# TensorE sums the first norm's squares, two end-gate outputs move into the first projection, and a modulation slab, the taps and two slab splits change places

## The chip, the cores and the metric

The kernel runs on one core of one Trainium2 chip. The metric is device time in microseconds (us), the median of several executions. Before the change it is 727.38 us, the median of three (727.26 to 727.83). The engines named below are TensorE (PE; PEld is its weight load), VectorE (DVE), ScalarE (ACT), GpSimd (POOL), and SyncE (SP), whose queue issues nearly all transfers.

## The reference, cut to what matters

Two stacks of two layers each run one after the other on x of 256 rows by 1024 columns, all in float32. The parts that the change touches are the first layer, the modulation vectors of the layers behind it, and the convolution with its layer norm in the second stack:

```python
shift, scale, gate = jnp.split(cs @ mod_w[layer] + mod_b[layer], 3, axis=-1)   # cs = silu(c)
h = _modulate(_rmsnorm(x, norm_g[layer]), shift, scale)        # the first norm: squares of x summed by row
u, g = jnp.split(h @ w_in, 2, axis=-1)                         # first projection u, end gates g
u = lax.conv_general_dilated(u, conv_w[:, None, :], ...) + conv_b          # 4 taps
r  = sigmoid(_block_diag(u, w_a) + b_a)                        # head gates
gi = sigmoid(_block_diag(u, w_x) + b_x)
log_a = -8 * r * softplus(-lam); a = exp(log_a)
b_in = sqrt(-expm1(2 * log_a)) * (gi * u)
_, hs = associative_scan(_lin_combine, (a, b_in), axis=1)
x = x + gate * ((hs * silu(g)) @ w_out)
# then: keys and values from x, queries and attention gates from x (second modulation), attention, output
# second stack, first layer (a Fourier mixer beside a gated convolution):
u = v * jax.nn.sigmoid(gate)
u = lax.conv_general_dilated(u, conv_w[:, None, :], ...) + conv_b          # 31 taps, 512 channels
u = silu(layernorm(u.reshape(b, s, 4, 128), ...))              # four channel tiles of 128
y = jnp.concatenate([ya, yb], axis=-1) @ w_out_ab
# then two gated feed-forward blocks (2816 wide) with a pooling mixer between them, and a last norm
```

## The kernel before, in words

A tile is 128 channels by 256 positions; x is eight of them (`X`). The program is written by hand, one instruction stream for each engine, with semaphores between them, and each stream runs in the order in which it is written. Nothing is scheduled by a tool.

**Weights.** They come as slabs of 1 MB or less (128 partitions by up to 2048 numbers) in the order of `PLAN`, which `slab_plan` (L19) writes. SP issues them in that order on one queue (L591 to L617). Slabs named in `OWN` (u, g, the two head matrices, y: the whole first layer) have places of their own. All others go through a ring of five buffers `raw`: a slab is issued only when the slab five places before it in the ring has been used up. While SP waits for that, all slabs behind it wait too. There are three kinds of ring slabs:
- "first": the two modulation vectors of the first layer. DVE multiplies the two halves of a slab with silu(c) and sums them (`first_sums`, L1071, two instructions over 1024 numbers each).
- "mod" (`MODS`): a piece of another modulation vector, read in the same way by `mod_sum` and `stream`. Numbers 0 to 3 are the first layer's output gate, 4 to 11 the keys' and values' modulation, 12 to 19 the query side's (alternately the factor and the shift), 20 to 23 the second layer's gate.
- matrices (`MATS`): each is split in a high and a low part. ACT copies it to the high part (L665), then DVE subtracts to get the low part (L1068, over 2048 numbers), and TensorE uses both in three products (L1638 to L1640). `stream(upto)` on ACT and on DVE works off the plan up to a slab at that place in the engine's own order; DVE does the mod slabs on its way, too.

**The first norm and the first projection.** ACT squares X into `F1` (L717 for four tiles, L720 for two and two). DVE adds the eight tiles to one (semaphore `s_n0`), TensorE sums that over its channels with two matmuls of one column (L1731), ACT takes the root, DVE the inverse (`c0`, L1197), TensorE spreads it over a tile (L1706), ACT copies it to `RS` (L665). Then, for each of the eight tiles kt, DVE multiplies X (`first_tile`), sums the "first" slab (`first_sums`) and closes it (`first_close`); ACT makes H(kt) (L728); TensorE uses H(kt) for all eight outputs u at once, with one slab for each kt (L1710). Matmuls on `ones`, whose results nobody reads, stand in the waits ahead (`idle_products`, L1715).
The end gates g 0 and 1 follow in banks of their own (`end_gates(0)`), then the head gates (16 outputs), the end gates 2 to 7, and the output projection y. Banks are given out in `outputs`. On DVE the softplus of lambda (`s_sp`), the 4-tap convolution (24 instructions, semaphore `s_conv`), the mod slabs 0 to 7, the recurrence, the mod slabs 8 to 11 and the first two matrix splits follow in that order. A head gate needs the convolution of its two tiles of u.

**Keys, values and queries.** DVE adds y to X tile by tile (L1071, `x<-pb,mv,x`) and gathers the squares for the second norm. TensorE starts the keys before that norm is known, and sums the norm's squares after the fourth kt of them (L1815), its inverse is spread after the sixth. Then come key inputs, value inputs and query inputs on ACT and DVE, between matrix splits and mod slabs.

**The convolution with 31 taps.** Three of its four channel tiles are made on DVE, 30 instructions each (`pump`, list `taps`; each reads and writes the same tile), the fourth on TensorE with diagonal matrices. Layer norm of the four tiles is done in steps between TensorE (`ln_mean`, `ln_var`, `ln_row`), ACT (`ln_square`, `ln_root`, `ln_high`) and DVE (`ln_centre`, `ln_inverse`, `ln_scale`, `ln_low`), tile 3 first. TensorE's product with `w_out_ab` (`mixed`, `both`) goes on between these steps as far as its inputs are there.

## Time and profile before

| | us |
|---|---|
| median of three runs | 727.38 |
| the profiled execution, own time | 727.91 |
| its span, first to last instruction | 726.1 |
| PE busy | 710.1 |
| PEld busy | 617.9 |
| DVE busy | 498.4 |
| ACT busy | 396.8 |
| POOL busy | 12.2 |
| longest chain, share that runs over PE / DVE | 81% / 14% |

The profiled execution took 1.8 us more than its span, for what lies around the program. The kernel moves 158.4 MB. A fp32 matmul is recorded as two instructions on PE, so a matmul of 256 columns has two records. The mean length of a matmul record says little, since matmuls overlap; the distance between starts is what counts.

### The profile page before, as it was taken

To read this page: it belongs to the slowest core of one execution; us is meant where nothing else is said; L and a number is where in the kernel's file an instruction comes from. 1 tells how busy PE (TensorE), PEld (TensorE's weight loads), DVE (VectorE), ACT (ScalarE), POOL (GpSimd) and SP (SyncE) were. 2 spreads that over 40 slices of the span, in tenths; PEclk is the share of its full clock that TensorE was granted. 3 is DMA by queue.
4 is the path that set the end of the run, shared out by engine and by line. 5 is a ranking of instruction groups with operands and counts; after the bars stand their busy time and mean duration, and the time that the engine had idled before them with its cause. 6 is when DMAs were issued, how large, how long until landed. Compare 5 with 4: busy or idle time off the path is not lost.

```text
span 726.1 us, 9536 instructions
## 1 busy us (share of the span) xinstructions
PE 710.1 (98%) x3812; PEld 617.9 (85%) x3812; DVE 498.4 (69%) x799; ACT 396.8 (55%) x616; POOL 12.2 (2%) x18
## 2 busy tenths in 40 slices
PE   6999999999999999989999999999999999999996
PEld 5888889979899999878888888888888888888885
DVE  5889996998877889966755454554776455454544
ACT  3156545964885778768643444334755443444423
POOL 0000000000310000000000000000000000000000
PEclk8999999999999999999999999999999999999999
DMA  8999994799836349433755455445236554455101
GB/s 334 416 421 422 420 400 164 250 388 341 352 117 232 118 174 265 142 116 135 287 211 178 175 196 205 178 174 181 109 116 231 196 203 181 176 190 207 67 1 58
DMA packets 23468, 158.40 MB, mean 218 GB/s; under 512 B 2624, under 2 KB 2880, under 8 KB 5248
## 3 DMA queue, kind: packets, MB, share of 16 engines
q1 hardware_dynamic: 22464, 152.82, 55.8%
q0 software_dynamic: 960, 4.98, 2.5%
q8 instruction: 30, 0.49, 0.3%
q14 instruction: 14, 0.11, 0.0%
HBM read 156.74 MB, written 1.05 MB: 217 GB/s over the span
## 4 chain that ended last, share of the span: by engine, by line
PE 81%; DVE 14%; ACT 2%; DMA 2%; issue 1%; SPq 0%; DVEq 0%
PE pb L1638 20%; PE pb L1640 20%; PE pb L1639 20%; PE pb L1710 13%; DVE f L1071 5%; DVE w L1068 3%; DVE raw L1071 3%; PE pb L2063 1%; DVE f L1068 1%; DMA raw<-w_dram 1%; PE pb L2131 1%; DVE r L1068 1%; PE pb L1985 1%; DMA x<-x_dram 1%; PE pb L1715 0%
## 5 line engine op out<-in xcount | busy, mean ns | idle before, releaser
L1068 DVE TENSOR_TENSOR w<-raw,w 128x2048 fp32r<-128x2048 f32 x95 | 216.9, 2290 | 141.4 <-ACT w L665 141.4
L665 ACT ACTIVATE w<-raw 128x2048 fp32r<-128x2048 f32 x99 | 188.5, 1914 | 144.9 <-PE pb L1640 114.7
L1638 PE MATMUL pb<-w,r 128*128 128x512 f32 (+1 forms) x608 | 238.9, 393 | 0.2 <-DVE r L1068 0.2
L1640 PE MATMUL pb<-w,r 128*128 128x512 f32 (+1 forms) x608 | 235.4, 387 | 0.0
L1639 PE MATMUL pb<-w,r 128*128 128x512 f32 (+1 forms) x608 | 235.0, 387 | 0.0
L1640 PEld LDWEIGHTS pb<-w,r 128*128 128x128 f32 x608 | 114.1, 188 | 23.7
L1638 PEld LDWEIGHTS pb<-w,r 128*128 128x128 f32 x608 | 114.2, 188 | 23.0 <-DVE r L1068 0.6
L1639 PEld LDWEIGHTS pb<-w,r 128*128 128x128 f32 x608 | 114.4, 188 | 22.2
L1638 PE MATMUL pb<-r,w 128*128 128x256 f32 x288 | 82.4, 286 | 1.5 <-DVE r L1068 1.0
L1640 PE MATMUL pb<-r,w 128*128 128x256 f32 x288 | 81.5, 283 | 0.0
L1639 PE MATMUL pb<-r,w 128*128 128x256 f32 x288 | 81.5, 283 | 0.0
L1071 DVE SCALAR_TENSOR_TENSOR raw<-raw,acc 128x1024 f32<-128x1024 f32 x64 | 75.1, 1219 | 4.0 <-DMA raw<-w_dram 4.0
L1638 PEld LDWEIGHTS pb<-r,w 128*128 128x128 f32 x288 | 55.2, 192 | 2.3 <-DVE w L1068 2.3
L1710 PE MATMUL pb<-h,ow 128*128 128x256 f32 x256 | 56.4, 383 | 0.0
L1710 PEld LDWEIGHTS pb<-h,ow 128*128 128x128 f32 x256 | 49.4, 193 | 7.0
L1639 PEld LDWEIGHTS pb<-r,w 128*128 128x128 f32 x288 | 55.2, 192 | 0.0
L1640 PEld LDWEIGHTS pb<-r,w 128*128 128x128 f32 x288 | 55.2, 192 | 0.0
L1002 ACT ACTIVATE t<-pb,rn 128x256 f32<-128x256 f32 x44 | 20.7, 476 | 59.7 <-PE pb L1640 59.6
L1071 DVE SCALAR_TENSOR_TENSOR f<-f,vec 128x256 f32<-128x256 f32 x114 | 46.4, 476 | 0.3
L1071 DVE SCALAR_TENSOR_TENSOR t<-pb,rn,t 128x256 f32<-128x256 f32 x44 | 21.1, 483 | 22.8 <-ACT t L1002 22.8
L1710 PE MATMUL pb<-t,ow 128*128 128x256 f32 x128 | 27.8, 379 | 0.0
L1710 PEld LDWEIGHTS pb<-t,ow 128*128 128x128 f32 x128 | 24.3, 190 | 3.3
(215 smaller groups left out, 667.4 us busy)
## 6 DMA issues: line engine op xcount, KB each, us to landing
raw<-w_dram SPq DMA_DIRECT2D x129, 1024.0 KB, 5.0
ow<-w_dram SPq DMA_DIRECT2D x8, 1024.0 KB, 14.8
ow<-w_dram SPq DMA_DIRECT2D x8, 512.0 KB, 16.5
oh<-w_dram SPq DMA_DIRECT2D x2, 1024.0 KB, 22.4
w<-w_dram POOLq DMA_DIRECT2D x2, 1024.0 KB, 14.5
x<-x_dram SPq DMA_DIRECT2D x2, 512.0 KB, 5.5
f<-rc_dram POOLq DMA_DIRECT2D x1, 1024.0 KB, 5.1
acc<-row_dram POOLq DMA_DIRECT2D x2, 512.0 KB, 4.8
```

Of the source, the lines that this page charges most:

```text
L665: return e.activation(out, in_, ACT.Copy, **kw)
L1002: e.activation(tt[(at_ - 1) % 4][:, :], bank_of("gu", layer, i, a)[:, 0:T], ACT.Silu, scale=rn[:, 2 * layer, a:a + 1]).then_inc(s_sgt, 1)
L1068: return e.tensor_tensor(out, a, b, op)
L1071: return e.scalar_tensor_tensor(out, a, s, b, op0, op1, **kw)
L1638: e.matmul(out, a_hi, b_hi, start=start, stop=False)
L1639: e.matmul(out, a_hi, b_lo, start=False, stop=False)
L1640: return e.matmul(out, a_lo, b_hi, start=False, stop=stop)
L1710: return e.matmul(out, slab[:, o:o + P], rhs, start=start, stop=stop)
L1985: done = e.transpose(bank_of("tx", n, a, m)[:, j * P:j * P + P], Xt[:, a, o:o + P], ident)
L2063: done = e.transpose(out[:, j * T + a * P:j * T + a * P + P], tt[4 + (at_ - 1) % 4][:, j * P:j * P + P], ident)
L2131: done = e.matmul(bank_of("p", a, c)[:, g % 2 * 256:g % 2 * 256 + 256], rc[:, b, g, a * P:a * P + P], Q[:, b, g, :], start=b == 0, stop=b ...
```

## The change

Five edits, all in the order of work; the arithmetic done on each weight stays the same.

1. The first norm: DVE's four additions of squares are gone (with `s_n0`). TensorE sums all eight squared tiles itself, with 16 matmuls of one column instead of 2; two of the idle matmuls ahead of it go. DVE takes the inverse before it sums the first "first" slab, not between that slab's halves, and the second half is summed behind `first_tile(0)`.
2. The slab of g 0 and 1 is cut in two parts. The part for kt 0 to 2 comes behind the third pair of slabs, and TensorE does these six matmuls behind kt 2 of the first projection; the part for kt 3 to 7 comes behind the last u slab, and its ten matmuls stand within kt 7, between the outputs u 5 and u 6. The outputs g 0 and g 1 lie in the free halves of the banks of u 6 and u 7. The head gates follow on u 7 at once.
3. The slab of mod 0 comes ahead of the two head matrices in the plan, and DVE sums it ahead of the 4-tap convolution.
4. The slabs of mod 12 and mod 13 come ahead of matrix slabs 2 and 3. DVE sums mod 12 ahead of the addition of y 7 and mod 13 ahead of matrix split 2; matrix split 3 is done before the wait for the second norm instead of behind the eight multiplications with it.
5. The 31 taps: the third tile's taps join the round of three from its third place on, so that at the end two taps on one tile stand in a row. `ln_inverse(3)` stands behind the eighth of the 15 taps that are left after `ln_centre(3)`, not behind all of them; `ln_scale(3)` and matrix split 28 come ahead of `ln_centre` of tiles 0 to 2. On TensorE the sums `ln_mean` of tiles 0 to 2 all stand behind `both(2)`.

```diff
@@ slab_plan
     for kt in range(KT):
         plan.extend([("first", "mod_w", 0, kt), ("u", "rg_w_in", 0, kt)])
-    plan.extend([("g", "rg_w_in", 0, 0), ("heads", "rg_w_a", 0), ("heads", "rg_w_x", 0)])
+        if kt == EARLY - 1:
+            plan.append(("part", "rg_w_in", 0, 0))
+    plan.append(("part", "rg_w_in", 0, EARLY))
+    at = len(plan)
     mod("mod_w", 0, 2)
+    plan[at + 1:at + 1] = [("heads", "rg_w_a", 0), ("heads", "rg_w_x", 0)]
...
-    weave(kv(512, D) + values + cols("att_w_in", 0, 512), [("mod", "mod_w", 1, unit, j) for j in range(4) for unit in (1, 0)],
-          [0, 2, 3, 3, 4, 5, 7, 7])
+    late = [("mod", "mod_w", 1, unit, j) for j in range(4) for unit in (1, 0)]
+    plan.extend(late[0:2])
+    weave(kv(512, D) + values + cols("att_w_in", 0, 512), late[2:], [3, 3, 4, 5, 7, 7])
@@ outputs
-    o.out(*run("u", *range(8)))
-    o.place(1, ("g", 0))
-    o.place(2, ("g", 1))
-    o.finish(("g", 0), ("g", 1))
-    rest = [3, 4, 5, 6, 7, 0]
+    o.hold(*run("u", *range(8)))
+    for b in range(2):
+        o.place(o.bank["u", 6 + b], ("g", b))
+    o.finish(*run("u", *range(6)))
+    o.finish(("g", 0), ("g", 1), ("u", 6), ("u", 7))
+    rest = [1, 2, 3, 4, 5, 6]
@@ taps
-        taps = [(d, j) for j in range(8) for d in (0, 1)]
-        taps += [x for j in range(8, 31) for x in ((0, j), (1, j), (2, j - 8))] + [(2, j) for j in range(23, 31)]
+        taps = [(d, j) for j in range(2) for d in (0, 1)]
+        taps += [x for j in range(2, 31) for x in ((0, j), (1, j), (2, j - 2))] + [(2, 29), (2, 30)]
@@ vector
-            two = F1[:, 0:2, :]
-            p.wait_ge(s_sq0, 1)
-            tt_(two, two, F1[:, 2:4, :], ADD).then_inc(s_n0, 1)
             for c in range(2):
                 p.wait_ge(*ended("sc", c))
                 e.tensor_copy(silu_c[:, c * 512:c * 512 + 512], bank_of("sc", c)[:, :]).then_inc(s_silu, 1)
-            for n in range(1, 3):
-                p.wait_ge(s_sq0, n + 1)
-                p.wait_ge(s_n0, n)
-                tt_(two, two, F1[:, 2 * n + 2:2 * n + 4, :], ADD).then_inc(s_n0, 1)
-            p.wait_ge(s_n0, 3)
-            tt_(F1[:, 0, :], F1[:, 0, :], F1[:, 1, :], ADD).then_inc(s_n0, 1)
+            p.wait_ge(s_rt, 1)
+            e.reciprocal(c0[:, :], c0[:, :]).then_inc(s_rc0, 1)
             p.wait_ge(s_xb, 16)
             first_sums(0, [0])
-            p.wait_ge(s_rt, 1)
-            e.reciprocal(c0[:, :], c0[:, :]).then_inc(s_rc0, 1)
-            first_sums(0, [1])
             p.wait_ge(s_rs, 1)
             first_tile(0)
+            first_sums(0, [1])
             first_close(0)
...
+            stream(MODS[0])
             p.wait_ge(s_pad, 1)
             for c in range(4):
...
-            stream(MODS[0])
+            stream(MODS[1])
             for d in range(8):
                 if d in (2, 4, 6):
-                    stream(MODS[d // 2])
+                    stream(MODS[1 + d // 2])
...
             for d in range(8):
+                if d == 7:
+                    stream(MODS[12])
                 p.wait_ge(*ended("y", d))
...
             add(7)
+            stream(MODS[13])
             stream(MATS[2])
             p.wait_ge(s_rt, 2)
             e.reciprocal(c1[:, :], c1[:, :]).then_inc(s_rc1, 1)
-            stream(MODS[12])
+            stream(MATS[3])
...
-            stream(MATS[3])
             key(0, 1, 2, 3)
...
-            stream(MODS[13])
             key(4, 5)
...
             pump(78 - tap_n["n"])
             ln_centre(3)
+            pump(8)
+            ln_inverse(3)
             pump(len(taps) - tap_n["n"])
-            ln_inverse(3)
+            ln_scale(3)
+            stream(MATS[28])
             ln_centre(0)
             ln_centre(1)
-            ln_scale(3)
-            stream(MATS[28])
+            ln_centre(2)
             ln_low(3)
-            ln_centre(2)
             stream(MATS[29])
@@ tensor
-            idle_products(4)
+            idle_products(2)
             bank_free("n", 0)
-            p.wait_ge(s_n0, 4)
-            for a in range(2):
-                done = e.matmul(bank_of("n", 0)[:, a:a + 1], F1[:, 0, a * P:a * P + P], ones_sb[:, 0:1], start=True,
-                                stop=True)
+            for kt in range(KT):
+                p.wait_ge(s_sq0, max(1, kt // 2))
+                for a in range(2):
+                    done = e.matmul(bank_of("n", 0)[:, a:a + 1], F1[:, kt, a * P:a * P + P], ones_sb[:, 0:1],
+                                    start=kt == a == 0, stop=kt == KT - 1 and a == 1)
...
+            def early_gates(part, kts):
+
+                slab, there = own("part", part)
+                p.wait_ge(*there)
+                for b in range(2):
+                    for kt in kts:
+                        done = plain(out_of("g", b), slab, (kt - part) * 256 + b * P, H(kt), False, False)
+                    if kts[-1] == KT - 1:
+                        done.then_inc(s_ps, 1)
...
                 for d in range(8):
+                    if kt == KT - 1 and d == 6:
+                        early_gates(EARLY, range(EARLY, KT))
...
+                if kt == EARLY - 1:
+                    early_gates(0, range(EARLY))
...
-            end_gates(0)
...
             both(1)
             ln_row(3)
-            ln_mean(0, (s_tap, tap_at[0, 30]))
-            ln_mean(1, (s_tap, tap_at[1, 30]))
             both(2)
+            for d in range(3):
+                ln_mean(d, (s_tap, tap_at[d, 30]))
             mixed(3, 0, 0, 1)
-            ln_mean(2, (s_tap, tap_at[2, 30]))
             mixed(3, 1, 0, 1)
```

What moves is seen in the order of DVE's instructions at three places. In these rows `raw,mv<-raw,acc ... x2` is the sum of one mod slab, `w<-raw,w` the low part of one matrix slab. First, around the 4-tap convolution (`f<-f,vec ... x24`), before and then now:

```order
51 L1227 TENSOR_SCALAR sm<-sm 128x8
52 L1228 TENSOR_SCALAR sm<-sm 128x8
53 L1071 SCALAR_TENSOR_TENSOR f<-f,vec 128x256 x24
54 L1071 SCALAR_TENSOR_TENSOR raw,mv<-raw,acc 128x1024 x2
55 L1068 TENSOR_TENSOR f<-f,t 128x256 x2
```

```order
48 L1230 TENSOR_SCALAR sm<-sm 128x8
49 L1231 TENSOR_SCALAR sm<-sm 128x8
50 L1083 SCALAR_TENSOR_TENSOR raw,mv<-raw,acc 128x1024 x2
51 L1083 SCALAR_TENSOR_TENSOR f<-f,vec 128x256 x24
52 L1083 SCALAR_TENSOR_TENSOR raw,mv<-raw,acc 128x1024 x2
53 L1080 TENSOR_TENSOR f<-f,t 128x256 x2
```

One mod slab is now summed ahead of the convolution. Second, from the end of the addition of y to the first multiplications with the second norm (`f<-x,rs`), before and then now:

```order
96 L1071 SCALAR_TENSOR_TENSOR r<-x,mv,kr 128x256
97 L1068 TENSOR_TENSOR na<-na,sq 128x256
98 L1071 SCALAR_TENSOR_TENSOR r<-x,mv,kr 128x256
99 L1068 TENSOR_TENSOR na<-na,sq 128x256
100 L1068 TENSOR_TENSOR w<-raw,w 128x2048
101 L1315 RECIPROCAL c<-c 128x2
102 L1071 SCALAR_TENSOR_TENSOR raw,mv<-raw,acc 128x1024 x2
103 L1068 TENSOR_TENSOR mv<-mv,vec 128x2
104 L1071 SCALAR_TENSOR_TENSOR mv<-mv,vec 128x2
105 L1068 TENSOR_TENSOR f<-x,rs 128x256 x8
106 L1068 TENSOR_TENSOR w<-raw,w 128x2048
```

```order
95 L1083 SCALAR_TENSOR_TENSOR mv<-mv,vec 128x2
96 L1083 SCALAR_TENSOR_TENSOR x<-pb,mv,x 128x256
97 L1083 SCALAR_TENSOR_TENSOR r<-x,mv,kr 128x256
98 L1080 TENSOR_TENSOR na<-na,sq 128x256
99 L1083 SCALAR_TENSOR_TENSOR r<-x,mv,kr 128x256
100 L1080 TENSOR_TENSOR na<-na,sq 128x256
101 L1083 SCALAR_TENSOR_TENSOR raw,mv<-raw,acc 128x1024 x2
102 L1080 TENSOR_TENSOR mv<-mv,vec 128x2
103 L1080 TENSOR_TENSOR w<-raw,w 128x2048
104 L1322 RECIPROCAL c<-c 128x2
105 L1080 TENSOR_TENSOR w<-raw,w 128x2048
106 L1080 TENSOR_TENSOR f<-x,rs 128x256 x8
```

Mod 12 (its last instruction is row 95) is ahead of the last addition, mod 13 ahead of the inverse, and a second split has come ahead of the eight multiplications. Third, the end of the taps and tile 3's layer norm (`lnr` is its inverse, `f<-pb,f` is `ln_centre`), before and then now:

```order
262 L1071 SCALAR_TENSOR_TENSOR f<-pb,f 128x256
263 L1071 SCALAR_TENSOR_TENSOR f<-f,vec 128x256 x15
264 L1488 RECIPROCAL lnr<-lnr 128x2
265 L1071 SCALAR_TENSOR_TENSOR f<-pb,f 128x256 x2
266 L1071 SCALAR_TENSOR_TENSOR f<-f,vec,pb 128x256
267 L1068 TENSOR_TENSOR w<-raw,w 128x2048
```

```order
260 L1083 SCALAR_TENSOR_TENSOR f<-pb,f 128x256
261 L1083 SCALAR_TENSOR_TENSOR f<-f,vec 128x256 x8
262 L1493 RECIPROCAL lnr<-lnr 128x2
263 L1083 SCALAR_TENSOR_TENSOR f<-f,vec 128x256 x7
264 L1083 SCALAR_TENSOR_TENSOR f<-f,vec,pb 128x256
265 L1080 TENSOR_TENSOR w<-raw,w 128x2048
266 L1083 SCALAR_TENSOR_TENSOR f<-pb,f 128x256 x3
```

The inverse has moved seven taps up.

## Rows read from the trace of the kernel before

**Rows 1.** The page, part 1: busy us, share of the span, instructions.
```profile
PE 710.1 (98%) x3812; PEld 617.9 (85%) x3812; DVE 498.4 (69%) x799; ACT 396.8 (55%) x616; POOL 12.2 (2%) x18
```

**Rows 2.** By stretch: length; PE, PEld, DVE, ACT, POOL busy; clock, DMA share, GB/s.
```profile
0.00:20.00 20.00, 14.12 (x49) 11.49 (x50) 12.13 (x30) 7.03 (x11) 0.19 (x4) 0.83 0.89 343
20.00:40.00 20.00, 20.00 (x95) 17.60 (x94) 15.82 (x38) 3.00 (x5) 0.00 (x0) 1.00 1.02 418
140.00:200.00 60.00, 58.02 (x392) 53.07 (x391) 56.01 (x100) 39.57 (x69) 5.89 (x6) 1.00 0.92 356
300.00:340.00 40.00, 38.01 (x196) 31.42 (x195) 30.50 (x65) 26.47 (x52) 0.53 (x1) 1.00 0.36 127
340.00:726.00 386.00, 379.94 (x1757) 315.60 (x1755) 209.80 (x203) 179.59 (x202) 0.00 (x0) 1.00 0.46 166
```

**Rows 3.** Timeline, 6 to 16 us: start, length, engine, line, operation [idle before].
```profile
6.73 1.06 ACT L717 ACTIVATE f<-x 128x1024 f32<-128x1024 f32 x1 [2.01 <-DMA x<-x_dram]
...
11.62 1.01 PE L1731 MATMUL pb<-ones_sb,f 128*128 128x1 f32 x4 [4.56 <-DVE f L1068]
...
12.67 0.26 ACT L722 ACTIVATE c<-pb,vec 128x2 f32<-128x2 f32 x1 [3.51 <-PE pb L1731]
...
15.29 0.60 ACT L728 ACTIVATE h<-f,mv 128x256 f32<-128x256 f32 x1 [0.76 <-DVE mv L1071]
```

**Rows 4.** Timeline of PEld, the same stretch.
```profile
11.62 0.93 PEld L1731 LDWEIGHTS pb<-ones_sb,f 128*128 128x128 f32 x4 [4.96 <-DVE f L1068]
...
16.05 1.19 PEld L1710 LDWEIGHTS pb<-h,ow 128*128 128x128 f32 x3
```

**Rows 5.** Busy time by 1 us, columns as in rows 2.
```profile
11.00:12.00 1.00, 0.38 (x2) 0.38 (x3) 0.97 (x3) 0.00 (x0) 0.00 (x0) 0.69 0.98 410
...
18.00:19.00 1.00, 1.00 (x5) 0.83 (x5) 1.00 (x4) 0.60 (x1) 0.00 (x0) 0.90 1.11 463
```

**Rows 6.** Timeline of PE at 318 us: matmuls of one column.
```profile
318.30 1.39 PE L1968 MATMUL pb<-ones_sb,t 128*128 128x1 f32 x12
```

**Rows 7.** Timeline of DVE, 37 to 56 us.
```profile
37.55 1.22 DVE L1071 SCALAR_TENSOR_TENSOR raw<-raw,acc 128x1024 f32<-128x1024 f32 x1 [0.74 <-DMA raw<-w_dram]
...
45.69 9.58 DVE L1071 SCALAR_TENSOR_TENSOR f<-f,vec 128x256 f32<-128x256 f32 x24
...
55.19 1.22 DVE L1071 SCALAR_TENSOR_TENSOR raw<-raw,acc 128x1024 f32<-128x1024 f32 x1
```

**Rows 8.** Timeline of PE at 51 us: the first head gates.
```profile
51.87 5.34 PE L1710 MATMUL pb<-f,oh 128*128 128x256 f32 x24
```

**Rows 9.** Timeline of DVE, 114 to 139 us.
```profile
114.23 0.48 DVE L1071 SCALAR_TENSOR_TENSOR x<-pb,mv,x 128x256 f32<-128x256 f32 x1 [2.24 <-PE pb L1710]
...
120.86 1.21 DVE L1071 SCALAR_TENSOR_TENSOR raw<-raw,acc 128x1024 f32<-128x1024 f32 x1
...
123.92 2.77 DVE L1068 TENSOR_TENSOR f<-x,rs 128x256 f32<-128x256 f32 x8 [0.31 <-ACT rs L665]
...
135.02 1.21 DVE L1071 SCALAR_TENSOR_TENSOR raw<-raw,acc 128x1024 f32<-128x1024 f32 x1
...
138.17 2.28 DVE L1068 TENSOR_TENSOR w<-raw,w 128x2048 fp32r<-128x2048 f32 x1
```

**Rows 10.** Timeline of ACT at 135 us: the high part of matrix slab 5.
```profile
135.47 1.90 ACT L665 ACTIVATE w<-raw 128x2048 fp32r<-128x2048 f32 x1
```

**Rows 11.** Timeline of PEld at 160 us: the first query weights.
```profile
160.69 0.19 PEld L1638 LDWEIGHTS pb<-r,w 128*128 128x128 f32 x1 [1.41 <-DVE w L1068]
```

**Rows 12.** Timeline of DVE, 272 to 312 us: taps, and tile 3's centre.
```profile
272.73 17.10 DVE L1071 SCALAR_TENSOR_TENSOR f<-f,vec 128x256 f32<-128x256 f32 x43
...
304.08 7.02 DVE L1071 SCALAR_TENSOR_TENSOR f<-f,vec 128x256 f32<-128x256 f32 x15
```

**Rows 13.** Timeline of ACT at 306 us: the root for tile 3.
```profile
306.60 0.26 ACT L945 ACTIVATE lnr<-pb,vec 128x2 f32<-128x2 f32 x1 [0.68 <-PE pb L1968]
```

**Rows 14.** Timeline of PE at 311 us: tile 3's row.
```profile
311.23 0.43 PE L1706 MATMUL pb<-cst,lnr 128*128 128x128 f32 x2 [1.80 <-DVE lnr L1488]
```

More of the change, by code:

```diff
@@ L15 @@
 RT = 8
+EARLY = 3
 def slab_plan():
@@ L97 @@
 PLAN = slab_plan()
-OWN = [i for i, p in enumerate(PLAN) if p[0] in ("u", "g", "y") or p[0] == "heads" and p[1] != "pool_map_2"]
+OWN = [i for i, p in enumerate(PLAN) if p[0] in ("u", "part", "g", "y") or p[0] == "heads" and p[1] != "pool_map_2"]
 RING = [i for i in range(len(PLAN)) if i not in OWN]
@@ L113, in width @@
 def width(i):
+    if PLAN[i][0] == "part":
+        return (KT - EARLY if PLAN[i][3] else EARLY) * 256
     return PLAN[i][4] * 256 if PLAN[i][0] == "mat" else D if PLAN[i][0] == "u" else 2048
@@ L403, in two_block_program @@
             sem(f"s_{n}") for n in ("ones", "pad", "gg", "cs", "silu", "lam", "sp", "one", "gain", "mv"))
-        s_sq0, s_n0, s_rc0 = sem("s_sq0"), sem("s_n0"), sem("s_rc0")
+        s_sq0, s_rc0 = sem("s_sq0"), sem("s_rc0")
         s_sq, s_na, s_rt, s_rs, s_rtc, s_rcl, s_rsb, s_xn = (
@@ L463, in two_block_program @@
             own_at["u", kt] = OW[:, kt // 4, kt % 4 // 2, o_:o_ + D]
+        own_at["part", 0] = OW[:, 2, 0, 0:EARLY * 256]
+        own_at["part", EARLY] = OW[:, 2, 0, EARLY * 256:2048]
         for c in range(4):
-            own_at["g", c] = OW[:, 2 + c // 2, c % 2, :]
+            if c:
+                own_at["g", c] = OW[:, 2 + c // 2, c % 2, :]
             own_at["y", c] = OW[:, c // 2, c % 2, :]
@@ L481, in out_of @@
         def out_of(*name):
+            if name in (("g", 0), ("g", 1)):
+                return PB[OUT.bank[name]][:, T:2 * T]
             return PB[OUT.bank[name]][:, 0:T]
@@ L2172 @@
     for i, p in enumerate(plan):
+        if p[0] == "part":
+            k0, k1 = (EARLY, KT) if p[3] else (0, EARLY)
+            m = a[p[1]][p[2]][k0 * P:k1 * P, D:D + 256]
+            w[i, :, 0:(k1 - k0) * 256] = m.reshape(k1 - k0, P, 256).transpose(1, 0, 2).reshape(P, -1)
+            continue
         if p[0] in ("first", "u", "g", "y"):
```

## The prediction

> **What bounds the kernel now.** I read the page first: TensorE is busy for 710.1 of 726.1 us [rows 1]. So an edit pays only if it shortens TensorE's work, which none of these does, or one of its 16 us of idle time. The busy time by stretch shows where they lie: 5.9 us in the first 20, 2.0 between 140 and 200, 2.0 between 300 and 340, 6.1 behind 340 [rows 2]. The last are the output's tail behind the last matmul and the change does not touch them. The timelines of the other three stretches tell what ends each idle time, and every edit lands in one of them.
> At the start TensorE waits 4.56 us for DVE's additions of squares, and its granted clock falls to half (mean 0.69 in 11 to 12 us, 0.90 in 18 to 19, so half from about 11.4 to 18.2 us) [rows 3, 5]. At 160 us it waits 1.41 us for a matrix split of DVE, which in 140 to 200 us is busy 56 of 60 us [rows 2, 11]. At 311 us it waits 1.80 us for the inverse that DVE makes behind 15 taps [rows 12, 14]. Between these places TensorE is never idle, so what is won at one is carried to the next.
>
> **Edit 1, the first norm.** The squares of the first four tiles are done at 7.79 us [rows 3]. DVE's additions go. TensorE has 16 matmuls of one column, 32 instructions. At full clock twelve such take 318.30 to about 319.56, 0.105 us each [rows 6], so 32 take 3.4 us; at half clock four loads take 0.8 us (0.93 with the last one's tail), 0.20 each, so 6.4 us [rows 4]. Those are the two ends. I take full clock, since the idle time ahead of them shrinks: TensorE was idle from 7.06 us; with two idle matmuls fewer (four instructions of about 0.22 us [rows 8]) it is idle from 6.2 to 7.8, that is 1.6 us in place of 4.56 [rows 3].
> The sum then ends at 11.4 instead of 12.63 us, the root at 11.7 instead of 12.93. But DVE now sums both halves of the first slab behind the inverse: inverse 0.1, half 1.15, tile 0.35, half 1.15 (a pair takes 2.30 [rows 7]), close and hand-over 0.5, so H(0) starts 3.3 us behind the root, at 15.0 instead of 15.29, and the projection's first weights at about 15.75 instead of 16.05 [rows 3, 4]. So most of the 1.2 us is given away in DVE's new order: 0.3 us.
> The clock has a price of its own: from 16.05 to 18.2 us the projection ran at half, which cost 1.1 us. Kept at full, that comes back too.
> The Trainium skill (TensorE: Matmul & The Clock Gate, Part 1) says that the slow clock is the default and that activity releases it. It does not say whether a stream of one-column matmuls counts as activity; if it does not, the first rival below holds.
>
> **Edit 2, the early gates.** The same 16 matmuls, 7.0 us (two instructions each, and 24 instructions take 5.34 us with the last one's tail, so 0.218 from start to start [rows 8]), stand within the projection. Six of them behind kt 2 give the later H tiles 2.6 us of room. Against that the part slab of 0.39 MB is now ahead of "first" slabs 3 to 7, and they come at the rate of the queue, 418 GB/s [rows 2]: 0.94 us later each. DVE waited for the last of them until 37.55 us [rows 7]; now until 38.5. H(7) is ready at 41.9, and TensorE comes to kt 7 at 15.75 + 7 x 3.48 + 2.6 = 42.7. No wait. It ends u 7 at 15.75 + 80 x 0.435 = 50.5 us.
> What follows now is the convolution, not the gates. Before it the gates g 0 and 1 hid it.
>
> **Edit 3, mod 0.** DVE's lambda work ends 0.94 us later, at 46.6. The slab of mod 0 has landed then: behind "first" 7 (38.5) come u 7, the second part slab and mod 0, 0.52 + 0.66 + 1.05 = 2.23 MB, at 418 GB/s until 43.8. It takes 2.30 us [rows 7], the convolution starts at 49.0 instead of 45.69 and its fifth instruction, which the first head gate needs, ends at 49.0 + 5 x 0.40 = 51.0 (24 take 9.58 [rows 7]). So the head gates start at 51.2, not 50.5: against 51.87 [rows 8] a gain of 0.5 to 0.65; I take 0.5. The head matrices land 2 x 2.5 us behind mod 0, at 48.8, 2.4 us ahead of their use. The ACT table for their sigmoids is loaded later, which costs nothing: six banks rotate and ACT needs 0.8 us less per pair than TensorE. On DVE mods 1 to 4 move up one place, so that the recurrence starts where it did, and y waits for nothing.
>
> **Edit 4, mods 12, 13 and split 3.** Before the addition of y 7 DVE idles 2.24 us [rows 9]. Mod 12 (2.5 us, from 135.02 to 138.17 less 0.67 for two multiplications [rows 9], with its small closing instructions 2.75) starts behind y 6 at about 111.4 and ends at 114.2: y 7 is added where it was, at 114.2. Mod 13 and split 2 run to 120.8, split 3 to 123.1, and the second norm's row, which hangs on TensorE alone, is there at 123.4 instead of 123.88: the eight multiplications start 0.5 us early with split 3 done [rows 9]. So 5 us of sums and 0.5 us of waits have left the stretch from 120.8 to 160. Not all counts. Split 5 needs ACT's high part, which started at 135.47 [rows 10] behind its key inputs; ACT's chain hangs on the norm's row, so it starts at 135.0 and ends at 136.9. DVE will wait there 2 us and end split 5 at 139.1 instead of 140.4. What follows (mods 14 to 17, splits 6 to 9) is one unbroken row of work on DVE, as before, 1.3 us early. Matrix slabs 7 and 8, for which ACT waited, are issued when split 5 and mod 15 are done, so they move along by 1.3. TensorE comes to 159.28 - 0.5 and gets its query weights at 160.69 - 1.3 = 159.4 [rows 11]. **Term A: 1.3 us.** Of it 0.5 is from the start (edits 1 to 3) and 0.8 from the reorder; the start alone would not be enough, since the wait of 1.41 would take it. In the attention stretch all goes in chains that start here, and behind 200 us TensorE is not idle until 309.
>
> **Edit 5, the taps and the inverse.** The first 43 taps take 17.0 us, 0.396 each; the last 15 take 6.94, since eight of them follow each other on one tile, 0.52 each [rows 12]. The root is there at 306.86 [rows 13]. Eight taps behind the centre (304.08 + 3.2) the inverse is at 307.3 to 307.4, and TensorE, which comes at 309.4, does not wait: 1.80 us [rows 14]. The seven taps left, two of them at 0.52, end at 310.5 instead of 311.0. What is late next? `ln_mean` comes at 312.4 and finds the taps done. DVE does the scale and split 28 to 313.1, the centres to 314.3 (they need the sums at 312.9, 313.4 and 313.8), low part and split 29 to 316.9. TensorE has two quarters of work until 316.4, then the variances: squares are done at 314.8. ACT's root table is loaded before them, where it was loaded beside them. Every step is 1.9 us early and none is the last by more than the old 0.2 us. **Term B: 1.9 us**, bounds 1.2 (a new wait of 0.7 at the row or the means) and 2.3.
> Behind 340 us TensorE is busy to the tail [rows 2], with DMA at 0.46, so both terms come through.
>
> **Sum.** 1.3 + 1.9 = 3.2 us. Against the profiled execution's own 727.91 (span 726.1 and 1.8 around it) 724.7. That execution was 0.53 us above the median 727.38, so the median becomes 724.2. Term A is 0.8 less the lateness of the head gates. Its bounds are -0.2 (the gates start 1.0 us late, for want of a slab or of the clock) and 2.2 (the first gates as computed, and DVE's wait of some 2 us ahead of split 5 is cut to half, since ACT's key inputs need not all come first). With B the likeliest case lies between 723.3 and 725.4.
>
> **The rivals.**
> 1. *The clock, on the slow side.* The one-column matmuls do not hold the clock, the sum runs at half and ends at 14.4; root and DVE's 3.3 us put the first weights at 18.65, 2.6 us later than before. If the clock then rises as late behind the start of wide work as it did (6.6 us behind 11.6 [rows 3, 5]), at 21.7, another 1.5 us are lost, and the head gates start at 55.0, 3.3 us late. TensorE is then the bound at 160, and DVE's reorder gives 0.8: 3.3 - 0.8 - 1.9 = +0.6, 728.0. It decides from a start of the head gates behind 54.4 us. For it: the clock did stay low for 5 us after work began at 11.6. Against: the idle time that came before the fall is cut to a third. Chance 4 in 100; with the sum at half and the clock up for the projection (head gates 2.0 late, so 2.0 - 0.8 - 1.9 = -0.7) 726.7, 7 in 100.
> 2. *The reorder is swallowed.* Something else ends the wait at 160: ACT's high parts 7 or 8 behind transfers that do not come sooner. Then A is 0.1, and the time is 727.4 - 0.1 - 1.9 = 725.4. For: DMA is at 0.92 in 140 to 200 us [rows 2]. Against: between 100 and 140 us the ring now frees earlier. 12 in 100.
> 3. *The layer norm's wait moves.* Taps and means meet the splits badly and B is 0.3: 727.4 - 1.3 - 0.3 = 725.8. For: six steps between three engines. Against: the margins above, 0.5 to 2 us each. 9 in 100.
> 4. *More than that.* ACT's part 5 is quicker, since its inputs are, and A is 2.2: 723.3. 8 in 100.
> 5. *The change does nothing*, because both waits are retaken: 727.3. 2 in 100.
>
> **The numbers.** The likeliest case holds 58 in 100, at 724.2. A difference of over 0.2% (1.45 us, so below 725.93 or above 728.83) is what a measurement tells from none. Faster: the case itself, 2 and 4, and two thirds of 3, together 84 in 100. Same: most of rival 1 (728.0 is slower than before, but by less than can be told), 5 and a third of 3, 13. Slower: what of rival 1 is worse than computed, 3. The range 722.9 to 726.0 leaves out the clock's cases, no change and a few above and below.
>
> **What would show it.** In the profile after: the one-column matmuls start near 7.85 us and end by 11.5, the clock stays at 1.00 through 20 us; DVE's convolution starts near 49.0 and the first head gate near 51.2; y 7's addition near 114.2 behind a mod sum without idle time; a wait of DVE of some 2 us ahead of split 5, the query weights at 159.4; no PE wait at the `lnr` row, and the last matmul 3.2 us early. I am wrong if the clock is at half in 8 to 18 us, if the query weights come after 160.3, or if TensorE waits over 0.5 us between 300 and 320.

## The result

| | before | changed |
|---|---|---|
| median, us | 727.16 | 725.07 |
| lowest to highest | 726.76 to 727.83 | 723.77 to 727.15 |
| executions | 14 | 14 |
| the profiled execution, own time | 727.91 | 724.46 |
| its span | 726.1 | 722.6 |

The ratio is 0.9972, with a 95% interval from 0.9964 to 0.9980: 2.1 us faster. 724.2 was forecast, with a range from 722.9 to 726.0. Two things don't fit yet. The profiled executions differ by 3.5 us and the medians by 2.1, and the changed kernel's times spread over 3.4 us where those before spread over 1.1. The spread by itself says little: beside the experiments the kernel before spread over 2.1 to 3.1 us.

The page, part 1, against [rows 1]:

```profile
PE 712.1 (99%) x3836; PEld 620.2 (86%) x3836; DVE 495.8 (69%) x795; ACT 397.2 (55%) x616; POOL 12.2 (2%) x18
```

Busy time by stretch, columns as in [rows 2]; the two rows of 1 us answer to [rows 5]:

```profile
0.00:20.00 20.00, 17.70 (x80) 15.09 (x81) 10.06 (x26) 7.03 (x11) 0.19 (x4) 0.91 0.89 342
20.00:40.00 20.00, 20.00 (x94) 17.62 (x93) 14.26 (x34) 3.00 (x5) 0.00 (x0) 1.00 1.02 416
140.00:200.00 60.00, 59.30 (x405) 54.87 (x405) 55.51 (x99) 41.12 (x72) 7.36 (x8) 1.00 0.90 348
300.00:340.00 40.00, 39.81 (x202) 33.07 (x201) 30.98 (x64) 29.16 (x55) 0.54 (x1) 1.00 0.32 119
...
11.00:12.00 1.00, 1.00 (x3) 0.69 (x4) 0.50 (x2) 0.26 (x1) 0.00 (x0) 0.50 1.08 438
...
18.00:19.00 1.00, 1.00 (x6) 0.87 (x6) 0.81 (x2) 0.60 (x1) 0.00 (x0) 1.00 1.04 425
```

TensorE's idle time in 140 to 200 us fell from 2.0 to 0.7 us, in 300 to 340 from 2.0 to 0.2. In the changed kernel's profile the clock was at half from 10.9 to 14.3 us, in the one before from about 11.4 to 18.2.

The start, from the timelines of ACT and PE, against [rows 3] and [rows 4]:

```profile
5.61 1.06 ACT L729 ACTIVATE f<-x 128x1024 f32<-128x1024 f32 x1 [0.87 <-DMA x<-x_dram]
...
15.11 0.60 ACT L740 ACTIVATE h<-f,mv 128x256 f32<-128x256 f32 x1 [2.03 <-DVE mv L1083]
```
```profile
7.45 3.72 PE L1738 MATMUL pb<-ones_sb,f 128*128 128x1 f32 x32
11.03 1.20 PE L1721 MATMUL pb<-sq,ones_sb 128*128 128x256 f32 x2
12.03 0.63 PE L1712 MATMUL pb<-cst,c 128*128 128x128 f32 x2
12.45 2.37 PE L1721 MATMUL pb<-sq,ones_sb 128*128 128x256 f32 x6
15.81 6.50 PE L1716 MATMUL pb<-h,ow 128*128 128x256 f32 x29 [0.99 <-issue]
```

The 32 one-column instructions took 3.72 us. H(0) starts at 15.11, as forecast (15.0), but X landed 1.12 us earlier here than in the profile before. Counted from the first square, H(0) came behind 9.50 us, and before behind 15.29 - 6.73 = 8.56. The edit made this chain longer, and an earlier transfer hid it.

DVE and TensorE up to the head gates, against [rows 7] and [rows 8]:

```profile
35.46 1.23 DVE L1083 SCALAR_TENSOR_TENSOR raw<-raw,acc 128x1024 f32<-128x1024 f32 x1 [1.67 <-DMA raw<-w_dram]
...
39.23 1.23 DVE L1083 SCALAR_TENSOR_TENSOR raw<-raw,acc 128x1024 f32<-128x1024 f32 x1 [0.74 <-DMA raw<-w_dram]
...
47.37 1.22 DVE L1083 SCALAR_TENSOR_TENSOR raw<-raw,acc 128x1024 f32<-128x1024 f32 x1
...
49.66 0.48 DVE L1083 SCALAR_TENSOR_TENSOR f<-f,vec 128x256 f32<-128x256 f32 x1
```
```profile
51.86 1.32 PE L1716 MATMUL pb<-f,oh 128*128 128x256 f32 x5 [1.08 <-DVE f L1083]
```

The last "first" slab is summed at 39.23 (37.55 before), so mod 0 runs at 47.37 and the convolution from 49.66. TensorE waits 1.08 us for it and starts the head gates at 51.86, where it started them before (51.87). The start has gained nothing.

DVE from y 7 to split 5, and the query weights, against [rows 9] and [rows 11]:

```profile
111.98 1.22 DVE L1083 SCALAR_TENSOR_TENSOR raw<-raw,acc 128x1024 f32<-128x1024 f32 x1
...
114.65 0.48 DVE L1083 SCALAR_TENSOR_TENSOR x<-pb,mv,x 128x256 f32<-128x256 f32 x1
...
123.99 2.77 DVE L1080 TENSOR_TENSOR f<-x,rs 128x256 f32<-128x256 f32 x8 [0.43 <-ACT rs L677]
...
137.47 2.29 DVE L1080 TENSOR_TENSOR w<-raw,w 128x2048 fp32r<-128x2048 f32 x1 [2.10 <-ACT w L677]
```
```profile
160.01 0.19 PEld L1644 LDWEIGHTS pb<-r,w 128*128 128x128 f32 x1 [0.72 <-DVE w L1080]
```

Mod 12 fills the 2.24 us ahead of y 7. Split 5 starts 0.70 us earlier than before, behind a wait of 2.10 us for ACT (2 were forecast), and the query weights come 0.68 us earlier.

The layer norm, against [rows 12] to [rows 14]:

```profile
302.53 3.25 DVE L1083 SCALAR_TENSOR_TENSOR f<-f,vec 128x256 f32<-128x256 f32 x8
305.69 0.16 DVE L1493 RECIPROCAL lnr<-lnr 128x2 f32<-128x2 f32 x1
305.77 3.09 DVE L1083 SCALAR_TENSOR_TENSOR f<-f,vec 128x256 f32<-128x256 f32 x7
...
311.37 1.26 DVE L1083 SCALAR_TENSOR_TENSOR f<-pb,f 128x256 f32<-128x256 f32 x3
```
```profile
307.72 0.38 PE L1712 MATMUL pb<-cst,lnr 128*128 128x128 f32 x2
```

The inverse is there 1.9 us ahead of its use, and the row of tile 3 is spread without a wait (1.80 us before). The 15 taps take 3.25 + 3.09 = 6.3 us instead of 7.0. Tile 3's row is 3.5 us earlier than before. Of that 1.6 had been won by the first of the 43 taps, which starts at 271.17 us where it started at 272.73.

### The profile page after: what moved, and what is told of

The parts are those of the page before. It is cut to its first block, busy times and chain, and to the rows that moved or that the text cites. A ratio compares the mean times of both kernels' runs of the same rounds, so it can differ in the third digit from the quotient of the medians.

```text
span 722.6 us, 9577 instructions
## 1 busy us (share of the span) xinstructions
PE 712.1 (99%) x3836; PEld 620.2 (86%) x3836; DVE 495.8 (69%) x795; ACT 397.2 (55%) x616; POOL 12.2 (2%) x18
## 4 chain that ended last, share of the span: by engine, by line
PE 81%; DVE 9%; DMA 4%; ACT 4%; SPq 1%; issue 0%; ACTq 0%
PE pb L1644 21%; PE pb L1646 21%; PE pb L1645 21%; PE pb L1716 9%; DMA raw<-w_dram 4%; DVE raw L1083 4%; DVE w L1080 3%; PE pb L1977 2%; PE pb L2082 1%; PE pb L2150 1%; PE pb L2005 1%; ACT t L795 1%; ACT r L792 1%; ACT w L677 1%; PE pb L1822 0%
```

## The experiments

All were timed in three groups, each beside the kernel before. Its medians were 727.30 us (19 executions; experiments 1 to 4), 727.43 (23; 5 to 8) and 727.50 (15; 9 to 12). A gain in us is the difference of the medians of one group. A ratio is to the kernel before, with its 95% interval, and isn't always the quotient of the medians.

**1. The fifth edit alone**, in the kernel before: lists of taps, `ln_inverse(3)` behind `pump(8)`, `ln_scale(3)` and split 28 ahead, `ln_mean` behind `both(2)`.

> The kernel before with the fifth edit alone (order of the taps, the inverse behind eight of fifteen taps, scale and split 28 ahead of the centres, the three means behind both(2)). My theory: the wait of 1.80 us for tile 3's inverse goes and nothing new stands in its place, so 1.9 us less than before, whatever the first 300 us do. Rival: the gain seen in the profile needs the 1.6 us that the other edits had won by 272 us; then the layer norm's wait moves and only 0.3 us are gained.

725.20 (724.51 to 725.48, 5 executions), ratio 0.9968 [0.9956, 0.9981]: 2.1 us. The row of tile 3 had no wait. The edit stands on its own, without what the others had won by 271 us, and the rival falls.

**2. The fourth edit alone**, in the kernel before.

```diff
+                if d == 7:
+                    stream(MODS[12])
...
+            stream(MODS[13])
             stream(MATS[2])
...
-            stream(MODS[12])
+            stream(MATS[3])
```

> The kernel before with the fourth edit alone (mods 12 and 13 ahead, matrix split 3 ahead of the second norm). My theory: 0.7 us at the query weights (160 us), as DVE's chain from split 5 on is 0.7 us early, and 0.9 us more at 187 us, where DVE's wait for late mod slabs was passed on to TensorE: together 1.6 us less than before. Rival A: the gain at 187 us came from the other edits (slabs issued earlier in the first 50 us), then 0.7 us. Rival B: the reorder is swallowed by transfers, then 0.1 us.

726.69 (725.74 to 727.93, 11), ratio 0.9992 [0.9983, 1.0001]: 0.6 us, not surely different from none by this alone. Its query weights:

```profile
160.09 0.19 PEld L1640 LDWEIGHTS pb<-r,w 128*128 128x128 f32 x1 [0.70 <-DVE w L1069]
```

The wait is 0.70 against 1.41 us, so the 0.7 us of the reorder are here. The 0.9 us at 187 us that I had added are not. The wait was in the profile before:

```profile
187.13 0.19 PEld L1638 LDWEIGHTS pb<-r,w 128*128 128x128 f32 x1 [0.89 <-DVE w L1068]
```

But the first experiment, which has the code of before up to there, did not have it either, nor had the twelfth; the eighth had 0.41 us of it. So it comes and goes with the execution. Rival A's size is right, though not by its cause.

**3. The first edit undone**, in the changed kernel.

```diff
+            two = F1[:, 0:2, :]
+            p.wait_ge(s_sq0, 1)
+            tt_(two, two, F1[:, 2:4, :], ADD).then_inc(s_n0, 1)
...
-            idle_products(2)
+            idle_products(4)
```

> The changed kernel with the first edit undone: DVE adds the squares again, two one-column matmuls, four idle products. My theory: the head gates wait for DVE's convolution at 51.9 us in either case, which hangs on the last first-layer slab's transfer, so the fastest executions are within 0.3 us of the changed kernel's; and if the one-column sums are what makes the changed kernel's times spread (3.4 us against 1.1 before), this kernel spreads by about 1 us again and its median is 0 to 0.7 us lower. Rival: the one-column sums are worth what was computed for them (0.3 us by the start and up to 1.1 us by the clock), and this kernel is 0.3 to 1.4 us slower than the changed one.

724.58 (724.25 to 724.97, 5), ratio 0.9961 [0.9947, 0.9975], 0.5 us below the changed kernel's median (0.6 counted from each one's own kernel before), spread 0.7 us in 5 executions. The intervals of the two ratios overlap, so the 0.5 is likely and not sure, and the fastest execution was 0.5 us slower than the changed kernel's, not within 0.3. The profiled execution happened to keep the full clock all the way, and shows what this chain takes then:

```profile
5.84 1.06 ACT L729 ACTIVATE f<-x 128x1024 f32<-128x1024 f32 x1 [1.08 <-DMA x<-x_dram]
...
13.66 0.60 ACT L740 ACTIVATE h<-f,mv 128x256 f32<-128x256 f32 x1 [0.86 <-DVE mv L1083]
```

H(0) comes 7.82 us behind the first square, against 9.50 with TensorE's sum. Yet the head start is lost at the head gates, which waited for the convolution:

```profile
51.59 5.63 PE L1725 MATMUL pb<-f,oh 128*128 128x256 f32 x25 [1.09 <-DVE f L1083]
```

**4. The second and third edits undone**, in the changed kernel: the slab of g 0 and 1 whole, `end_gates(0)` behind the projection, mod 0 behind the convolution.

> The changed kernel with the second and third edits undone: end gates 0 and 1 behind the whole first projection again, mod 0 behind the 4-tap convolution. My theory: those two edits cost time, because the convolution starts at 49.7 instead of about 45.7 us and nothing is left to cover it; without them TensorE works from 15.8 us on without a gap and comes to the head gates at 50.6 to 50.9 instead of 51.86, so 1.0 us less than the changed kernel, some 3.1 us less than before in the median. Rival: early gates are needed, because otherwise TensorE waits for H(4) to H(7) behind the transfers; then 0.5 us slower than the changed kernel.

725.58 (724.53 to 728.01, 9), ratio 0.9974 [0.9962, 0.9987]: 1.7 us, where the changed kernel has 2.1. The theory, 1.0 us less than the changed kernel, missed. The rival's number came out, 0.5 us more, but its cause isn't seen: TensorE waited for no H tile. In this profiled execution the clock fell inside the one-column matmuls. First PE's timeline, then the busy time of 8 to 9 and 9 to 10 us:

```profile
7.70 6.32 PE L1726 MATMUL pb<-ones_sb,f 128*128 128x1 f32 x32 [1.26 <-ACT f L718]
...
18.65 3.71 PE L1704 MATMUL pb<-h,ow 128*128 128x256 f32 x16 [0.58 <-issue]
```
```profile
8.00:9.00 1.00, 1.00 (x9) 1.00 (x8) 0.00 (x0) 0.57 (x2) 0.00 (x0) 0.73 0.96 393
9.00:10.00 1.00, 1.00 (x6) 1.00 (x7) 0.00 (x0) 0.58 (x2) 0.00 (x0) 0.50 1.03 381
```

The 32 instructions took 6.32 us, 0.20 each, and the projection started at 18.65 us, as in the forecast's first rival (6.4 and 18.65), in the branch in which the clock is up for the projection: it was at 1.00 from 19 us on. The head gates started at 53.28, without a wait of TensorE. An execution at full clock, which the theory was about, wasn't profiled.

**5. The convolution first**: mod 0 behind it again, the rest as changed.

```diff
-            stream(MODS[0])
             p.wait_ge(s_pad, 1)
...
-            stream(MODS[1])
+            stream(MODS[0])
```

> The changed kernel with mod 0 summed behind the 4-tap convolution again (its slab stays ahead of the head matrices, the early gates stay). My theory: the head gates waited 1.08 us for DVE's convolution only because 2.3 us of mod sum stand ahead of it; now the convolution starts at 47.3 and the gates at 50.8, and 0.5 to 1.0 us come off the changed kernel's median (executions in which the clock falls at the start gain nothing, since TensorE is the bound there). Rival: the mod sums behind the convolution are late for the recurrence and the wait comes back before the output projection: no gain.

726.07 (723.52 to 728.42, 11), ratio 0.9979 [0.9966, 0.9991]. Neither theory: the fastest execution is 0.25 us below the changed kernel's fastest, but the median is 1 us above its median (0.7 counted from each one's own kernel before). Eight of the eleven executions had a mean clock of 0.991 or less, and there the time is: 723.5 at 0.995, 726.0 to 726.4 at 0.990 and 0.991, 727.5 to 728.4 at 0.988. In its profile the clock was at half from 11.4 to 21.7 us, and the head gates started at 53.89 without a wait for DVE.

**6. A wide sum**: 8 matmuls of 256 columns.

```diff
-                for a in range(2):
-                    done = e.matmul(bank_of("n", 0)[:, a:a + 1], F1[:, kt, a * P:a * P + P], ones_sb[:, 0:1],
-                                    start=kt == a == 0, stop=kt == KT - 1 and a == 1)
+                done = e.matmul(out_of("n", 0), ones, F1[:, kt, :], start=kt == 0, stop=kt == KT - 1)
...
-            e.reciprocal(c0[:, :], c0[:, :]).then_inc(s_rc0, 1)
+            e.reciprocal(RS[0][:, :], RS[0][:, :]).then_inc(s_rs, 1)
```

> The changed kernel, but TensorE sums the squares with 8 matmuls of 256 columns with the ones as weights (same number of squares, the result stands in all 128 partitions, so the two spreading matmuls and ACT's copy go, and ACT's root and DVE's inverse are made over 256 columns); 6 idle products behind it instead of 1 and 3. My theory: it is the one-column matmuls in which the granted clock falls (from 10.9 us in the changed kernel, from 8.7 us in the fourth experiment); with wide ones it stays at 1.00, the times spread by about 1 us instead of 3.4, and the median is 0.5 to 0.8 us below the changed kernel's, at 724.4. Rival: the clock falls at the start in some executions whatever TensorE does there, and the spread stays at 3 us.

726.15 (724.77 to 731.37, 12), ratio 0.9984 [0.9969, 0.9999]. A miss, but by a new cause. The sum itself took the same 3.72 us with the clock at 1.00. Then DVE's inverse over 256 columns took 1.75 us, H(0) came 10.11 us behind the first square, and TensorE ran out of idle products. The clock fell 0.8 us after the end of that gap (0.52 in 18 to 19 us). First DVE's inverse, then TensorE's gap:

```profile
11.74 1.75 DVE L1194 RECIPROCAL rs<-rs 128x256 f32<-128x256 f32 x1 [5.60 <-ACT rs L732]
...
17.18 5.16 PE L1712 MATMUL pb<-h,ow 128*128 128x256 f32 x15 [3.40 <-issue]
```

The 731.37 stands beside a clock of 0.990, but 726.1 and 726.3 stand beside 0.997; what made those slow isn't known. So the spread, 6.6 us, didn't shrink with the wide sum, as the theory had it.

**7. Wide sum and convolution first**, and the first half of the first slab ahead of the inverse.

> Both together, and the first half of the first slab summed ahead of the inverse. If the two gains are independent, 1.5 us below the changed kernel, at 723.6. If they are not (the start is bound by the transfers of the first-layer slabs either way), it is no better than the better of the two.

724.12 (724.09 to 725.60, 5), ratio 0.9959 [0.9946, 0.9972]. Head gates at 50.86 us with no wait of TensorE, clocks 0.995 to 0.999. That is 3.3 us less than before and 2 us below both of its parts. The forecast for independent gains was 723.6. Which of the changes does it can't be told, since the half slab ahead of the inverse is a third one.

**8. DVE's additions and convolution first**: the third experiment with the edit of the fifth.

> The third experiment (squares added by DVE, as before) with mod 0 behind the convolution. Without the convolution as the cover, the head gates hang on TensorE: 50.5 us in an execution at full clock, 51.5 to 51.9 in one where the clock falls in the wait for DVE. Median 0 to 1.0 us below the third experiment's 724.6, with a wider spread than its 0.7. Rival: no change, since something else ends last at 51.5.

724.76 (724.38 to 726.00, 5), ratio 0.9965 [0.9953, 0.9977], no different from the third's, where 0 to 1.0 us less was expected. Its profiled execution, the slowest of the five, started the head gates at 51.51 with the clock at half from 10.7 to 17.6 us and no wait for DVE: there TensorE was the bound, and the fallen clock cost as much as the convolution had in the third.

**9. The fourth and fifth edits only**, in the kernel before.

> The kernel before with the fourth and fifth edits alone. Theory: the gains of the first and second experiments add up (2.1 + 0.6), median 724.6, and since the third experiment (which has the second and third edits on top) had 724.6 too, those two edits are worth nothing. Rival: the early gates and the earlier mod 0 are worth 0.5 us, as was forecast; then 725.1 here.

724.69 (724.02 to 725.04, 5), ratio 0.9956 [0.9943, 0.9970]: 2.8 us, the sum of the first two experiments (2.1 + 0.6), and as fast as the third, which has edits 2 and 3 on top. So beside DVE's additions these two show no gain. The changed kernel (2.1 us) seems to lose 0.7 us to its first three edits; its interval, 0.9964 to 0.9980, and this one's still overlap, so the loss isn't certain. Beside the one-column sum edits 2 and 3 look better by 0.4 us (2.1 in the changed kernel, 1.7 in the fourth experiment), which is within the noise too.

**10. The wait filled**: the third experiment with `idle_products(10)` for `idle_products(4)`.

> The third experiment (squares added by DVE) with 10 idle products in place of 4 ahead of the sum, so that TensorE, idle there from 7.9 to 10.7 us, works through. Theory of the idle time (the clock falls because TensorE was idle): it stays at 1.00 in every execution (mean clock 0.997 or more), and the median is 0.3 to 0.5 us below the third experiment's. Rival: the clock falls whatever TensorE does (it fell in the changed kernel behind 3.5 us of unbroken one-column work); then no change, or 0.2 us slower where a product delays the sum.

724.89 (724.54 to 725.23, 5), ratio 0.9960 [0.9947, 0.9972]. Four of the five clocks are 0.997 or more, of the third experiment's only one, but no time came off: the head gates waited 1.10 us for the convolution, as in the third. The 0.3 to 0.5 us that were expected did not come.

**11. The wide sum, filled**: the seventh with 12 idle products for 6.

> The seventh experiment with 12 idle products behind the sum in place of 6, so that the 2.95 us ahead of the projection are filled with wide work. If idle time is what lets the clock fall, mean clocks stay at 0.997 or more and the median is 723.8 to 724.1 with a spread under 1 us; if the seventh's times were good by chance, this one spreads like the sixth (over 3 us).

724.14 (723.52 to 724.73, 5), ratio 0.9950 [0.9937, 0.9962]: 3.4 us, with clocks of 0.997 and 0.998 and a spread of 1.2 us. It is no different from the seventh (3.3 us); these two are the fastest. PE's timeline of the start:

```profile
7.24 3.72 PE L1732 MATMUL pb<-f,ones_sb 128*128 128x256 f32 x16 [0.71 <-ACT f L727]
10.80 5.34 PE L1716 MATMUL pb<-sq,ones_sb 128*128 128x256 f32 x24
16.38 5.85 PE L1711 MATMUL pb<-h,ow 128*128 128x256 f32 x26 [0.24 <-issue]
```

The projection starts 0.57 us later than in the changed kernel's profile, yet at full clock and with nothing to wait for, and the head gates start at 50.99.

**12. The first edit alone**, in the kernel before.

> The kernel before with the first edit alone (one-column matmuls). Theory: mean clocks of 0.988 to 0.991 come with this edit, in a third or more of the executions, and these are slower than before by 0.5 us or more (before's wait of 1.41 us at 160 us takes up the rest); median 727.0 to 728.0, and a spread of 2 us or more in the same call in which the ninth has about 1. Rival: the low clocks need the other edits too, and this kernel's clocks are those of before (0.993 to 0.997), its median 0.3 us lower.

727.77 (727.21 to 730.36, 11), ratio 1.0007 [0.9997, 1.0017], no gain, and 0.3 us slower by the medians. Four of eleven executions had clocks of 0.989 to 0.991; they took 728.35 to 730.36. The low clocks come with this edit and need no other. The 0.3 us is within the interval; what is clear is that executions with the low clock are slow. In its profile, of an execution with a mean clock of 0.994, the clock went to half while TensorE worked without a gap through the one-column matmuls:

```profile
9.00:10.00 1.00, 1.00 (x11) 1.00 (x10) 0.00 (x0) 0.49 (x1) 0.00 (x0) 1.00 1.01 397
10.00:11.00 1.00, 1.00 (x8) 1.00 (x8) 0.00 (x0) 0.00 (x0) 0.00 (x0) 0.69 0.98 352
11.00:12.00 1.00, 1.00 (x6) 1.00 (x6) 0.00 (x0) 0.00 (x0) 0.00 (x0) 0.50 1.02 426
```

### The runs side by side

From the first square to H(0), in the profiled executions:

| who sums the squares | clock | us |
|---|---|---|
| DVE (before, experiments 1, 2, 8, 9) | half from about 11 us | 8.56 or 8.57 in all five |
| DVE (3, 10) | full | 7.82 in both |
| TensorE, one column (changed, 5, 12) | half from 10.9, 11.4, 10.4 us | 9.50, 9.16, 9.70 |
| TensorE, one column (4) | half from 8.5 us | 11.36 |
| TensorE, 256 columns (6, 7, 11) | full | 10.11, 9.29, 9.55 |

Mean clock of 0.991 or less: 19 of 45 executions of the four kernels with the one-column sum (4 of 14, 3 of 9, 8 of 11, 4 of 11 for changed, 4, 5 and 12), and none of 93 with DVE's additions (57 of the kernel before beside the experiments, 36 of experiments 1, 2, 3, 8, 9 and 10). The edit also took two idle products away ahead of the sum. That this was the cause, and not the one-column work, is unlikely: experiments 6, 7 and 11 have the same two and the wide sum, and of their 22 executions one had such a clock (0.990, the 731.37). A one-column sum behind four or more idle products wasn't run. In the changed kernel the four such executions took 726.15 us on average and the five of 0.994 or more 724.57.

From the start of the head gates to the end of the span: 670.7 us in the changed kernel, 671.1, 670.6, 670.7, 670.9, 670.9 and 671.0 in experiments 3, 4, 5, 6, 9 and 10, whose head gates start anywhere from 51.59 to 53.89. (7 and 11 have 671.4 and 671.2; 8 has 672.7, with 2.15 us of idle time of TensorE in 140 to 200 us in place of 0.7.) So in the first seven of these profiles what was won or lost ahead of the head gates reached the end one to one; in 7 and 11 some 0.5 us was lost on the way, in 8 some 2 us.

## Why the prediction was right, and where it was wrong

**The value.** 724.2 was forecast, 725.07 measured, inside the range and faster, as given at 84 in 100. The gain is the harder test: 3.2 us were forecast (727.4 - 724.2) and 2.1 came. Term B was right, the larger part of term A (0.8 of 1.3) was right, the rest failed. The prediction had named three signs of being wrong. One came true, the clock at half between 8 and 18 us; the other two did not (query weights after 160.3 us: they came at 160.01; over 0.5 us of waiting between 300 and 320 us: TensorE's idle time in 300 to 340 was 0.2).

**Edit 5, term B, 1.9 us: right.** 2.1 by the first experiment. In the profile the stage gained 3.5 - 1.6 = 1.9. The steps came as written: the inverse behind eight taps, no wait at the row, the taps 0.7 us shorter, and TensorE's sums for the variances (318.30 before, 314.78 now) as much earlier as the row.

**Edit 4, 0.8 of term A: right.** 0.7 at the query weights (waits of 0.70 to 0.72 us in the changed kernel, 2 and 9, against 1.41 before), 0.6 by the median of the second experiment, whose interval includes no gain. The wait moved from DVE's split to ACT ahead of split 5, as said: 2.10 us where about 2 was written. Split 5 started 0.7 earlier and not 1.3, because ACT's chain hangs on the norm's row, hence on TensorE, and TensorE had won nothing at the start. So rival 2 did not happen, nor rival 3 or 4.

**Edits 1 to 3, 0.5 of term A: wrong.** Two steps failed.

The first is "I take full clock, since the idle time ahead of them shrinks". The idle time did shrink (TensorE had none between 5.7 and 14.8 us in the changed kernel's profile), and the clock fell all the same, at 10.9 us. Even in the best of the profiles the sum of one-column matmuls didn't pay: 9.16 us from the first square to H(0), against 8.56 with DVE's additions at a fallen clock. Counted in the same way, the forecast had 15.0 - 6.73 = 8.27. That H(0) started at 15.11 us where 15.0 was forecast is luck: the transfer of X was 1.12 us early. In the changed kernel the sum started 1.84 us behind the first square instead of 1.12, since idle products left in the queue ran to 7.6 us though the squares were there at 6.67; it took 3.72 us instead of 3.4; and with the clock at half for what followed that makes 9.50. And 8.27 was held against the wrong number: before was read from an execution with a fallen clock, and the same chain takes 7.82 us at the full clock that I assumed for the changed kernel. By the medians the edit costs 0.3 us alone (12) and 0.5 in the changed kernel (against 3), neither of them surely more than nothing.

The second is the sum for the convolution. The last "first" slab was reckoned 0.94 us later and came 1.68 later. That is no accident of one execution: DVE starts on it at 38.72 to 40.44 us (39.38 on average) in the eight profiles that have edit 2, and at 37.44 to 38.11 (37.81) in the six that haven't, so the part slab ahead costs some 1.6 us and not 0.94. Why it costs more than its bytes at 418 GB/s stays open. The kt 7 weights at 42.74 were right (42.7). The convolution was due at 49.0 and came at 49.66, so the gates came at 51.86 instead of 51.2: the margin of 0.65 us was all used by slabs that came 0.7 us late. I had seen that "what follows now is the convolution, not the gates" and did not list it as a rival of its own. Against the ninth experiment, the third shows no gain from edits 2 and 3 in the median.

**Rival 1, the clock: too small a chance, and too little of a case.** I gave it 11 in 100 as one outcome for the kernel. It is an outcome for the execution: about 4 in 10 of those with the one-column sum have a low mean clock, and 4 of 14 in the changed kernel itself. The fourth experiment's profile met its numbers for the sum and the projection. Its numbers for the head gates, 2.0 and 3.3 us late, don't follow from its own terms: weights at 18.65 and 80 steps of 0.435 give 53.5 us, and 55.0 with the clock, so 1.6 and 3.1 late against 51.87; the profile had 53.28. It did not turn the verdict, since edits 4 and 5 carry 2.8 us.

**Why 3.5 us in the profiles and 2.1 in the medians.** The changed kernel's profiled execution was faster than most (724.46 at a clock of 0.996), that of before slower than its 14 timed ones (727.91 against 726.76 to 727.83), in part by the 0.89 us at 187 us, which the first experiment, with the same code up to there, did not show.

**The balance.** Edits 4 and 5 gain 2.8 us together (2.1 and 0.6 alone), and the changed kernel has 2.1. The missing 0.7 us is put down to edit 1, which loses 0.3 alone and 0.5 in the changed kernel; the rest is within the noise.

## What to carry to other kernels

Measure a chain from its own trigger (here X's arrival) to its end, not by the clock of the trace: an earlier transfer made a longer chain end sooner. When work is moved to an engine whose clock depends on what it does, count the result as a distribution over executions and look at the clock of each. And when a hidden step is put ahead of another on a second engine, its margin has to be larger than the lateness of the transfers that feed it.

## What the runs showed of the hardware

- Unbroken work of one-column matmuls did not keep TensorE at 2.4 GHz: it went to 1.2 GHz while they ran, 0.8 us behind their start in experiment 4, 2.6 in 12, 3.4 in the changed kernel and 3.2 in 5. A wide sum in their place was at full clock in all three profiles that have it (6, 7, 11). Experiments 4 and 6 came to the sum behind nearly the same idle time, 1.26 and 1.36 us: in 4 the clock fell while the sum ran, in 6 it did not. With DVE's sum the clock stayed up through idle times of 1.99 (10) and 2.82 us (3), and fell during those of 2.83 (2), 2.93 (1), 3.13 (8), 4.56 (before) and 4.73 us (9), one execution each; 2.82 and 2.83 stand on either side, so the length of the idle time alone does not decide it. The Trainium skill (TensorE: Matmul & The Clock Gate, Part 1) calls the slow clock the default and says that how much work runs cold differs from execution to execution of one kernel. The second is what the mean clocks show (0.988 to 0.997 for one kernel); of one-column work it says nothing.
- 32 instructions of one-column fp32 matmuls took 3.72 us mostly at full clock (0.12 each, changed kernel) and 6.32 at half (0.20 each, experiment 4). Sixteen instructions of 256 columns took the same 3.72 us at full clock (6, 7, 11), so this wide sum cost TensorE no more than the narrow one.
- DVE's inverse of 128x256 took 1.75 us (6), against 0.42 for a multiplication of the same size (6) and 0.17 for an inverse of 128x2 (changed kernel).
